# A chunked RWKV-7 recurrence on one core: two products that share a moving operand, made as one with a 128-column stationary operand

## What is computed

```
def step(S, inp):                      # per token, S is (heads, v, k)
    r_t, w_t, k_t, v_t, kk_t, a_t = inp
    sa = einsum('bhvk,bhk->bhv', S, kk_t)
    S = S * w_t - sa[..., None] * (kk_t * a_t) + v_t[..., None] * k_t
    y = einsum('bhvk,bhk->bhv', S, r_t)
```

## Time and profile before

| | |
|---|---|
| three runs | 2504.36, 2505.54, 2509.64 us; median 2505.54 us |
| the profiled execution's own time | 2510.38 us |
| its span, first to last instruction | 2508.6 us |
| mean granted TensorE clock | 0.980 |
| PE busy | 2392.6 us, 95% |
| PEld busy | 2278.2 us, 91% |
| DVE busy | 1511.0 us, 60% |
| ACT busy | 1183.1 us, 47% |
| the recurrence | about 508 to 585 us of the span |

### The profile page before, as it was taken

How to read it: one execution, slowest core, us unless ns; L and a number is a source line. 1 busy time by engine, 2 the same in 40 slices (tenths; PEclk the granted TensorE clock), 3 DMA queues, 4 the chain that set the end, 5 groups by cost and what they waited for, 6 DMA issues and landing times.

```text
span 2508.6 us, 49280 instructions
## 1 busy us (share of the span) xinstructions
PE 2392.6 (95%) x20449; PEld 2278.2 (91%) x20449; DVE 1511.0 (60%) x1825; ACT 1183.1 (47%) x1496; POOL 19.1 (1%) x35
## 2 busy tenths in 40 slices
PE   7999997986999999999899999999999999999998
PEld 7999997876989899999899999999999888999886
DVE  7587556656574445555879895554855444555444
ACT  4587353133354446664754345446545433444342
POOL 0000000000000000000000000000000000000000
PEclk9999999998999999999999999999999999999999
DMA  8355567303545564455466565555566666666554
GB/s 256 119 176 174 172 182 205 102 22 133 180 159 184 188 182 142 152 191 182 129 182 177 168 183 163 168 168 185 156 192 184 186 189 185 185 184 186 188 187 134
DMA packets 234516, 425.06 MB, mean 169 GB/s; under 512 B 34256, under 2 KB 36640, under 8 KB 233616
## 3 DMA queue, kind: packets, MB, share of 16 engines
q1 hardware_dynamic: 207232, 397.46, 51.5%
q10 hardware_dynamic: 24448, 12.82, 2.1%
q0 software_dynamic: 2656, 12.17, 1.6%
HBM read 413.48 MB, written 8.91 MB: 168 GB/s over the span
## 4 chain that ended last, share of the span: by engine, by line
PE 85%; DVE 8%; ACT 3%; issue 2%; DMA 2%; ACTq 1%; SPq 0%; DVEq 0%
PE ps L489 26%; PE ps L490 25%; PE ps L491 25%; PE ps L695 2%; DVE wlo L350 2%; ACT whi L346 1%; PE ps L602 1%; PE ps L703 1%; PE ps L616 1%; DMA regions<-in_a_a 1%; DMA ab_scratch<-regions 0%; DMA regions<-in_xT 0%; DVE regions L1783 0%; DVE act_lo L1965 0%; PE ps L881 0%
## 5 line engine op out<-in xcount | busy, mean ns | idle before, releaser
L350 DVE TENSOR_TENSOR wlo<-wraw,whi 128x1024 fp32r<-128x1024 f32 x752 | 917.4, 1224 | 896.7 <-ACT whi L346 895.6
L489 PE MATMUL ps<-act_hi,whi 128*128 128x256 f32 (+1 forms) x4736 | 1359.7, 287 | 54.0 <-DVE wlo L350 13.0
L490 PE MATMUL ps<-act_lo,whi 128*128 128x256 f32 (+1 forms) x4736 | 1342.1, 283 | 0.0
L491 PE MATMUL ps<-act_hi,wlo 128*128 128x256 f32 (+1 forms) x4736 | 1340.8, 283 | 0.0
L346 ACT ACTIVATE whi<-wraw 128x1024 fp32r<-128x1024 f32 x752 | 793.6, 1059 | 1130.3 <-PE ps L491 1095.8
L489 PEld LDWEIGHTS ps<-act_hi,whi 128*128 128x128 f32 x4736 | 901.4, 190 | 60.9 <-issue 36.2
L490 PEld LDWEIGHTS ps<-act_lo,whi 128*128 128x128 f32 x4736 | 904.3, 191 | 1.3
L491 PEld LDWEIGHTS ps<-act_hi,wlo 128*128 128x128 f32 x4736 | 901.2, 190 | 0.0
L491 PE MATMUL ps<-whi,regions_r 128*128 128x512 f32 x512 | 203.0, 396 | 0.0
L490 PE MATMUL ps<-wlo,regions_r 128*128 128x512 f32 x512 | 203.0, 396 | 0.0
L489 PE MATMUL ps<-whi,regions_r 128*128 128x512 f32 x512 | 203.0, 396 | 0.0
(11 more groups left out here) (316 smaller groups left out, 1395.3 us busy)
## 6 DMA issues: line engine op xcount, KB each, us to landing
wraw<-in_a_w_in SPq DMA_DIRECT2D x128, 512.0 KB, 3.8
wraw<-in_w_up SPq DMA_DIRECT2D x128, 512.0 KB, 3.9
wraw<-in_w_down SPq DMA_DIRECT2D x128, 512.0 KB, 4.3
wraw<-in_w_in SPq DMA_DIRECT2D x112, 512.0 KB, 3.8
wraw<-in_b_w_qg SPq DMA_DIRECT2D x64, 512.0 KB, 3.8
wraw<-in_a_w_out SPq DMA_DIRECT2D x32, 512.0 KB, 3.9
wraw<-in_w_k_shared SPq DMA_DIRECT2D x32, 512.0 KB, 4.4
wraw<-in_w_v_shared SPq DMA_DIRECT2D x32, 512.0 KB, 4.3
```

Of the source, the lines that this page charges most:

```text
L350: nc.vector.tensor_tensor(wlo[:, q % RING], wraw[:, q % RING], whi[:, q % RING].bitcast(F32), ALU.subtract).then_inc(lo_ready, 1)
L489: mm(o, hi_s, hi_m, start=first, stop=False, skip_group_check=True)
L490: mm(o, hi_s, lo_m, start=False, stop=False, skip_group_check=True)
L491: i = mm(o, lo_s, hi_m, start=False, stop=last, skip_group_check=True)
```

## The change

Three things go together.

- **Layout.** KR becomes tile, chunk, a, token, with a swapped for odd tiles, so that the two streams of one tile and chunk are 128 adjacent columns. The scan is made per chunk (64 scans of 64 elements instead of 16 of 256), and the operations that cover four tiles of one stream become two, one for each parity.
- **Products.** The two value products are one, with 64 rows and 128 columns stationary, and so are the two state products. Value products alternate between row halves (p inside), state products take all of f=0, then all of f=1. The result of each lies in bank 4p+f: W on the partitions of side(p), y on those of the other side.
- **Copies.** W and y are taken out in halves of 64 partitions: four ACT copies each where there were two. In the last chunk one y half of each f goes to DVE. The order of `am`, masked keys and transposes is changed, and the value products wait for all four ACT copies of BKt.

```diff
-                into_tokens((0, 1), 0, key(Bc, it), chan(KR, 1, ts), sig=S["am_mm"])
-                for n_ in range(2):
-                    if n_ and it:
-                        pe.wait_ge(S["y_sb"], 2 * it)
+                def masked_keys(n_):
...
-                            m_ = mm(ps[side(p), 2 + 2 * n_ + f, (i % 4) * P:(i % 4 + 1) * P].rearrange("p (a t) -> p a t", a=2),
-                                    Kc[side(f), i, it, p, :], KR[side(f), 2 * i + p, :, ts], start=True, stop=True)
+                            m_ = mm(ps[side(p), 2 + 2 * n_ + f, (i % 4) * P:(i % 4 + 1) * P],
+                                    Kc[side(f), i, it, p, :], KR[side(f), 2 * i + p, it].rearrange("k a t -> k (a t)"), start=True, stop=True)
...
+                masked_keys(0)
+                if it:
+                    pe.wait_ge(S["y_sb"], 4 * it - 1)
+                into_tokens((0, 1), 0, key(Bc, it), decay(1, it), sig=S["am_mm"])
+                if it:
+                    pe.wait_ge(S["y_sb"], 4 * it)
+                masked_keys(1)
                 if it < 3:
                     pe.wait_ge(S["am_ready"], 6 * it + 2)
+                    turn(Kc, 2)
+                    pe.wait_ge(S["am_ready"], 6 * it + 4)
                     turn(Bc, 0)
-                    pe.wait_ge(S["am_ready"], 6 * it + 4)
-                    turn(Kc, 2)
                 pe.wait_ge(S["am_ready"], 6 * it + 6)
+                if it < 3:
+                    pe.wait_ge(S["tok_ready"], 4 * it + 4)
                 for f in range(2):
-                    if it < 3:
-                        pe.wait_ge(S["tok_ready"], 4 * it + f + 1)
-                    m_ = within_tokens(f, f, am(1), value, last=it == 0)
+                    for i, p in SLOTS:
+                        m_ = mm(ps[:, 4 * p + f, cols(i)], AM[side(p), 8 * f + i, 1:3, :].rearrange("k a t -> k (a t)"), value(f, i, p),
+                                start=i == 0, stop=False, skip_group_check=True)
                     m_.then_inc(S["first_mm"] if it else S["w_mm"], 1)
-                for f in range(2):
-                    within_tokens(f, 4 + f, am(2), value, last=False).then_inc(S["first_mm"], 1)
                 if it:
                     pe.wait_ge(S["m_sb"], 2 * it)
-                    pe.wait_ge(S["first_mm"], 4 * it)
-                    into_tokens((0, 1), 0, chan(KR, 0, ts), state, first=False, sig=S["w_mm"])
-                    pe.wait_ge(S["first_mm"], 4 * it + 2)
-                    into_tokens((0, 1), 4, chan(KR, 1, ts), state, first=False, last=False, sig=S["state_mm"])
+                    pe.wait_ge(S["first_mm"], 2 * it)
+                    for f in range(2):
+                        for i, p in SLOTS:
+                            m_ = mm(ps[:, 4 * p + f, cols(i)], KR[side(f), 2 * i + p, it].rearrange("k a t -> k (a t)"), state(f, i, p),
+                                    start=False, stop=False, skip_group_check=True)
+                        m_.then_inc(S["w_mm"], 1)
                 if it < 3:
-                    pe.wait_ge(S["tok_ready"], 4 * it + 4)
                     into_channels(6, tok(1), value, last=False)
                 for f in range(2):
-                    pe.wait_ge(S["w_sb"], 2 * it + f + 1)
+                    pe.wait_ge(S["w_sb"], 4 * it + 2 * f + 2)
                     within_tokens(f, 2 + f, flat(TTs[:, it]), flat(Wt)).then_inc(S["u_mm"], 1)
...
-                within_tokens(0, 4, am(0), flat(U), first=False).then_inc(S["y_mm"], 1)
+                inner(0)
...
# ScalarE
-                    st.do(a(Wt[:, f * GW:(f + 1) * GW], bank(f), ACT.Copy), sig["w_sb"])
+                    for p in range(2):
+                        st.do(a(Wt[side(p), f * GW:(f + 1) * GW], ps[side(p), 4 * p + f, :], ACT.Copy), sig["w_sb"])
...
-                    st.do(a(Yn[:, it, :].rearrange("p (i f n) -> p i f n", f=2, n=N)[:, :, f, :],
-                            bank(4 + f).rearrange("p (i n) -> p i n", n=N), ACT.Copy), sig["y_sb"])
+                    for p in range(2 if it < 3 else 1):
+                        st.do(a(*taken_y(it, f, p), ACT.Copy), sig["y_sb"])
# VectorE
-                    st.do(nc.vector.tensor_tensor_scan(KR[:, j, 1, :], cs("restart"), KR[:, j, 0, :], 0.0, ALU.mult, ALU.add),
-                          sig["dec_done"] if j == KT - 1 else None)
+                    for c in range(4):
+                        st.do(nc.vector.tensor_tensor_scan(decays(1, j)[:, c, :], cs("ones")[:, 0:CH], decays(0, j)[:, c, :], 0.0, ALU.mult,
+                                                           ALU.add), sig["dec_done"] if j == KT - 1 and c == 3 else None)
...
+            for f in range(2):
+                dve.wait_ge(S["y_mm"], 7 + f)
+                st.do(nc.vector.tensor_copy(*taken_y(3, f, 1)))
```

More of the change, by code:

```diff
@@ L812, in _, with inner @@
                 for f in range(2):
-                    pe.wait_ge(S["w_sb"], 2 * it + f + 1)
+                    pe.wait_ge(S["w_sb"], 4 * it + 2 * f + 2)
                     within_tokens(f, 2 + f, flat(TTs[:, it]), flat(Wt)).then_inc(S["u_mm"], 1)
+                def inner(f):
+                    for i, p in SLOTS:
+                        m_ = mm(ps[side(1 - p), 4 * p + f, cols(i)], AM[side(p), 8 * f + i, 0, :], flat(U)(f, i, p), start=False, stop=True,
+                                skip_group_check=True)
+                    m_.then_inc(S["y_mm"], 1)
@@ L1114, in sigmoids @@
                     for j in (2 * j2, 2 * j2 + 1):
-                        st.do(a(chunks(KR[:, j, 0, :]) if i == 0 else tile_of(Bc, j), chunks(ps[:, 4 + n_ % 4, (j % 2) * T:(j % 2 + 1) * T]), ACT.Sigmoid,
+                        st.do(a(decays(0, j) if i == 0 else tile_of(Bc, j), chunks(ps[:, 4 + n_ % 4, (j % 2) * T:(j % 2 + 1) * T]), ACT.Sigmoid,
                                 bias=ve("w0" if i == 0 else "a0", j)), sig["lora_s1"])
@@ L1140, in key_part @@
                 j4 = slice(4 * g, 4 * g + 4)
-                cum = KR[:, j4, 1, :]
                 if w == 0:
@@ L1144, in key_part @@
                         act.wait_ge(S["kp_dve"], 2 * g - 1)
-                    for i in range(2):
-                        st.do(a(as_tiles(by_two(tmpA[2], 2)[:, i]), in_tiles(cum[:, 2 * i:2 * i + 2, :]), ACT.Exp, scale=DECAY),
-                              sig["kp_act"] if i else None)
+                    for p in range(2):
+                        st.do(a(by_two(tmpA[2], 2)[:, :, :, p, :], of_parity(1, g, p), ACT.Exp, scale=DECAY), sig["kp_act"] if p else None)
                 if w == 1:
-                    st.do(a(KR[:, j4, 0, 1:T], KR[:, j4, 1, 0:T - 1], ACT.Exp, scale=-DECAY), sig["kp_act"])
+                    for p in range(2):
+                        st.do(a(of_parity(0, g, p)[:, :, :, 1:CH], of_parity(1, g, p)[:, :, :, 0:CH - 1], ACT.Exp, scale=-DECAY),
+                              sig["kp_act"] if p else None)
                 if w == 2:
@@ L1163, in key_part @@
                     act.wait_ge(S["kp_act"], 3 * g + 2)
-                    st.do(a(cum, cum, ACT.Exp, scale=-DECAY), sig["gi_ready"])
+                    for p in range(2):
+                        st.do(a(of_parity(1, g, p), of_parity(1, g, p), ACT.Exp, scale=-DECAY), sig["gi_ready"] if p else None)
             def spread_rn(g):
@@ L1266, in _ @@
                         act.wait_ge(S["m_mm"], 2 * it)
-                    st.do(a(BKt[:, u // 2, 4 * (u % 2):4 * (u % 2) + 4, :], bank(u).rearrange("p (i m) -> p i m", i=4), ACT.Copy), sig["tok_ready"])
+                    st.do(a(BKt[:, 1 - u // 2, 4 * (u % 2):4 * (u % 2) + 4, :], bank((2, 3, 0, 1)[u]).rearrange("p (i m) -> p i m", i=4), ACT.Copy), sig["tok_ready"])
                 for f in range(2):
                     act.wait_ge(S["w_mm"], 2 * it + f + 1)
-                    st.do(a(Wt[:, f * GW:(f + 1) * GW], bank(f), ACT.Copy), sig["w_sb"])
+                    for p in range(2):
+                        st.do(a(Wt[side(p), f * GW:(f + 1) * GW], ps[side(p), 4 * p + f, :], ACT.Copy), sig["w_sb"])
                 if it:
@@ L1671, in key_part @@
                     dve.wait_ge(S["kp_act"], 3 * g + 2)
-                    st.do(nc.vector.memset(KR[:, j4, 0, 0::CH], 1.0))
+                    for p in range(2):
+                        st.do(nc.vector.memset(of_parity(0, g, p)[:, :, :, 0], 1.0))
                     st.prev()
                     for j in range(4 * g, 4 * g + 4):
-                        st.do(stt(chunks(KR[:, j, 0, :]), tile_of(Kc, j), ve("k_k", j), chunks(KR[:, j, 0, :]), ALU.mult, ALU.mult))
+                        st.do(stt(decays(0, j), tile_of(Kc, j), ve("k_k", j), decays(0, j), ALU.mult, ALU.mult))
                 if w == 2:
@@ L1700, in _ @@
                 dve.wait_ge(S["gi_ready"], s + 1)
-                st.do(tt(KR[:, j4, 1, :], KR[:, j4, 1, :], ps[:, 2 * (s % 2):2 * (s % 2) + 2, :].rearrange("p b (c t) -> p (b c) t", c=2), ALU.mult),
-                      sig["acc_free_dve"])
+                for p in range(2):
```

(2 more changed lines are left out.)

49 lines of the change are left out of this document (27 added, 22 removed).

## The result

The changed kernel takes 2537.84 us (median of four runs, 2535.01 to 2540.08) against 2506.68 us: 1.0125 times the time of before, 95% interval 1.0109 to 1.0141, so some 31 us slower where 12 were forecast, and outside the range of 2499 to 2534 us. The profiled execution, the shortest of the four, took 2535.01 us, 24.6 more than the profiled one of before (2510.38). The two profiles thus show some 25 of the 31 us.

What follows compares the result with a forecast made beforehand. In the recurrence PE's own pace plus its pauses, read as waits for instructions, were taken as the bound; terms of -1.0, +12.0, -2.0, +2.5, +0.5 and +0.1 summed to +12.1 us, giving 2517.6 us, range 2499 to 2534.

Steps and rivals of the forecast that it cites:

- the load's price: Merged products on PE: a pair with a 64-row, 128-column load costs 112 ns, set by its columns; bounds 60 and 112.
- rival B: Merged products: a 64-row load is as quick with 128 columns as with 64, 60 ns a pair; 2500.9 us, chance 0.20.
- rival D: Merged value products: the two row halves don't load together, +14 us more, 2532 us; chance 0.06.
- the wait for the BKt copies: Before the value products, chunks 0 to 2: PE waits 0.87 us longer for all four ACT copies, +2.5 us.
- the scans: Slab steps in group k: 12 added starts at 0.08 us, 0.9 us a step, hidden in DVE's idle 1.01 us.
- the state products' term: State products, three chunks: 64 pairs at 112 ns, 7.2 us a chunk, 21.5 for 9.5 now, +12.0 us; the deciding term.
- rival C: State products: granted clock falls with one row half working, 1.7 to 7.2 us a chunk, +10 more, 2528 us; chance 0.14.
- A: Whole kernel: the forecast's own sum of terms, +12.1 us, alone 2511 to 2523 us; chance 0.60.
- The last chunk keeps its dip of the clock: Value products of chunk 3: the lower clock level lasts 3.4 us as before, so they take 5.2 us.
- the value term: Merged value products: 3.6 us a chunk, 5.2 in the last, 16.0 in sum for 17.0 now, -1.0 us.
- the pauses elsewhere: PE's instruction pauses outside value and state products, 7.9 us: one of 0.7 us fewer in three chunks, -2.0 us, bounds 0 and -4.
- W in halves in chunk 3: Two more ACT copies a chunk, uncovered in chunk 3, where no channel products follow: +0.5 us.

Runs made afterwards that it cites:

- experiment 4: The changed kernel with each state product streaming 128 columns of M instead of 64; 2528.76 us in one run beside 2508.3 for the kernel before.
- experiment 9: The kernel before with 64 already fulfilled waits added to PE's program at the start of chunk 1; 2511.30 us in one run beside 2506.55.

## Why the prediction was right or wrong

**Right: the direction, and the load's price.** The decisive term was named with its place, and the 112 ns a pair were 110 at the full clock (experiment 4). The record of a load was 183 to 188 ns at the full clock there, as with 96 and 128 rows and 128 columns; rival B, break-even at 74 ns, was wrong. The estimate by the rule of the Trainium skill (TensorE: Matmul & The Clock Gate, section LDWEIGHTS) was 107 ns, nearly as close; the trace, with 110, agrees within 3 ns at the full clock, and at the lower clock the record of a load is 330 ns.

**Right: the value products' pace at the full clock** (3.79 us for 3.6), so rival D was wrong: the row halves load together. **Right: the wait for the BKt copies**, 2.6 us for 2.5. **Right: the scans** in group k are hidden: sixteen take 3.02 us where 3.3 were allowed (0.05 us for each added start, where I took 0.08 without a row), and DVE still idles 0.39 us before its next slab:

```profile
98.30 3.02 DVE L1670 TENSOR_TENSOR_SCAN regions<-cst,regions 128x64 f32<-128x64 f32 x16
101.71 1.23 DVE L356 TENSOR_TENSOR wlo<-wraw,whi 128x1024 fp32r<-128x1024 f32 x1 [0.39 <-ACT whi L352]
```

**Wrong: the state products' term, +12.0 us, which was +24.7.** This is the step that failed: 64 pairs at 112 ns in each of three chunks took the full clock as given. At the lower clock a pair took about twice as long, 13.09 us for the 64 of chunk 3, and the stretches took 10.4, 10.8 and 13.1 us instead of 7.2. In chunks 1 and 2 rival C was true on top of A: the clock fell some 3 us into the state products. Against C I had set that PE pauses 1.40 us in chunk 1 while the clock of the chunk is 1.00, and that evidence did not bear on it. A pause of 1.4 us inside dense work says little about a stretch of 7 us in which each load leaves the matmul idle for half of its time. The argument for C, about half of the work that PE does now, stood in the same paragraph, with a chance of 0.14. In chunk 3 another premise failed, "The last chunk keeps its dip of the clock": the clock was down already when the state products began, and did not come back after 3.4 us but after 20.

**Wrong: C's price, "something between" 1.7 and 7.2 us a chunk.** The state stretches lost 3.4, 3.8 and 6.1 us against 7.0, 13 in all where C had 10. And the lower clock does not end with them: it held through the channel products and into the solve of chunks 1 and 2 (1.98 us for 1.1, 2.5 and 3.3 us for 2.0) and through the solve of chunk 3 (3.1 for 2.05). That is 4 to 5 us more, for which C had no term. C's sum also missed the value products' 3 us and, the other way, the 4 us of pauses below. In sum the recurrence grew by 26.5 us where C's terms give 22. That the medians lie 31 us apart, and 2537.84 so far above C's 2528, is in part the spread of the runs.

**Wrong: the value term, -1.0 us.** In chunk 3 they took 4.53 + 1.66 us and a pause of 1.39 for what I took at 5.2: the clock was down for all of the 4.53 us. In sum the group is 17.6 us of work plus 1.4, some 2 us more than before where I had 1 less.

**Off: the pauses elsewhere, -2.0 us.** They went from 7.9 to 1.5 (0.8 and 0.7), -6.4, beyond my bound of -4. I had expected one fewer a chunk. That slow products let the instructions catch up nearly everywhere fits, but no run tests it.

**Off: W in halves in chunk 3, +0.5 us**, did not show: PE goes from the state products to the solve (603.74) without a pause.

## What to carry to other kernels

Before two small products are merged into one with a wider stationary operand, count loads by their columns and ask which parts of the array could load side by side: here two 64-column loads side by side on one row half took 56 ns together (3.6 us for 64 times two), one 128-column load 110. If they are merged all the same, write the loop so that consecutive products alternate between row halves: here that was the difference between 3.8 and 10.4 us for the same 64 pairs. Ask also where the matmul is much shorter than its load for microseconds on end: here the clock then fell to its lower level, and the work behind was slow too. And price what follows a wait at both levels of the clock: in the profile of chunk 3 it stayed down for 3.4 us or less with 64 x 64 value products, for 10 us or more with merged ones.

## What the runs showed of the hardware that was not expected

- Streaming twice the columns through the same loads made a stretch faster: 7.0 us against 10.4, since the granted clock stayed at 1.00.
- A copy of 64 partitions on ACT costs as much as one of 128: 591 ns for the 64x512 copies of W, where the 128x512 ones of before took 595 on average.

```profile
L1290 ACT ACTIVATE work<-ps 64x512 f32<-64x512 f32 x16 | 9.5, 591 | 53.0 <-PE ps L819 50.0 <-PE ps L811 2.8
```

- 64 waits that were long fulfilled held PE for 3.30 us, at most some 50 ns each, named issue in the profile (experiment 9):

```profile
526.55 1.98 PE L703 MATMUL ps<-regions 64*64 64x64 f32 x64 [3.30 <-issue]
```

- A clock that is up is kept by products that don't bring it back once it is down. The merged value products keep it at 1.00 in chunks 1 and 2 of every profile that has them; in chunk 3 they ran at the lower level for 4 to 7 us without its return, and the 128-column state products of experiment 4 kept 1.00 for 7.0 us in chunks 1 and 2 and stayed at 0.50 for 13.3 us in chunk 3.
- Why the clock behind the masks is back after 3.4 us with 64 x 64 value products (or does not fall, experiment 9) and after 10 us or more with merged ones is open. No run separates the form of the products from the moment at which they start, and chunk 0, where the clock fell in three of five profiles of the same work, shows that the moment counts for something.
